# FFN up projection of a two-block model: weights or tokens as the standing operand

## The reference

```python
h = rms_norm(x, ln_ffn_pre[i])                 # (256, 2048)
g, u = jnp.split(h @ w_gate_up[i], 2, axis=-1) # w_gate_up: (2048, 2 * 5632)
f = (jax.nn.silu(g) * u) @ w_down[i]           # w_down: (5632, 2048)
x = x + rms_norm(f, ln_ffn_post[i])
```

## Time and profile before

| what | value |
|---|---|
| median of 3 runs | 2859.03 us (2858.27 to 2859.66) |
| the profiled execution's own time | 2858.7 us |
| its span in the profile | 2856.9 us |
| PE busy | 2817.7 us, 99% |
| PE weight loads (beside the matmuls) | 2400.2 us, 84% |
| DVE busy | 1732.5 us, 61% |
| ACT busy | 1284.7 us, 45% |
| GpSimd busy | 123.8 us, 4% |
| HBM read | 511.49 MB, 180 GB/s over the span |

### The profile page before, as it was taken

How to read it: one execution, slowest core, us unless ns; L and a number is a source line. 1 busy time by engine, 2 the same in 40 slices (tenths; PEclk the granted TensorE clock), 3 DMA queues, 4 the chain that set the end, 5 groups by cost and what they waited for, 6 DMA issues and landing times.

```text
span 2856.9 us, 40648 instructions
## 1 busy us (share of the span) xinstructions
PE 2817.7 (99%) x14485; PEld 2400.2 (84%) x14485; DVE 1732.5 (61%) x2253; ACT 1284.7 (45%) x1818; POOL 123.8 (4%) x129
## 2 busy tenths in 40 slices
PE   6999999999999999999999999999999999999999
PEld 3678888888888899988888999998888888888887
DVE  4468888888763366644456666675645555544465
ACT  3422224343352254434445677674544444444463
POOL 0000001001010000001112000000000000000000
PEclk9999999999999999999999999999999999999999
DMA  9765565445645245533335555555555555566655
GB/s 384 284 218 185 185 222 178 161 163 179 218 133 184 96 161 179 180 123 110 110 111 163 175 165 177 164 177 188 170 187 189 191 185 190 191 201 193 194 180 170
DMA packets 144780, 515.27 MB, mean 180 GB/s; under 512 B 16768, under 2 KB 16824, under 8 KB 142752
## 3 DMA queue, kind: packets, MB, share of 16 engines
q1 hardware_dynamic: 141408, 496.84, 52.2%
q0 software_dynamic: 3264, 16.94, 1.7%
HBM read 511.49 MB, written 2.22 MB: 180 GB/s over the span
## 4 chain that ended last, share of the span: by engine, by line
PE 95%; DVE 2%; ACT 1%; issue 1%; DMA 1%; POOL 0%; SPq 0%; DVEq 0%; ACTq 0%; POOLq 0%
PE main L1994 70%; PE main L1987 16%; PE aux L1941 2%; PE main L2300 2%; PE aux L2197 1%; PE aux L2188 1%; PE aux L2300 1%; PE aux L2316 1%; PE aux L2248 0%; DVE w_lo L1203 0%; DMA X<-in_xT 0%; PE main L2412 0%; DVE scores L1758 0%; DMA wide<-in_w_side 0%; PE aux L2200 0%
## 5 line engine op out<-in xcount | busy, mean ns | idle before, releaser
L1203 DVE TENSOR_TENSOR w_lo<-raw,w_hi 128x1024 fp32r<-128x1024 f32 (+1 forms) x768 | 924.4, 1206 | 768.2 <-ACT w_hi L677 759.2
L677 ACT ACTIVATE w_hi<-raw 128x1024 fp32r<-128x1024 f32 (+1 forms) x768 | 788.1, 1030 | 1180.3 <-PE main L1994 922.8
L1994 PE MATMUL main<-w_hi,act_hi 128*128 128x512 f32 (+1 forms) x1408 | 530.6, 377 | 2.9 <-DVE scores L1485 1.5
L1994 PE MATMUL main<-w_hi,act_lo 128*128 128x512 f32 (+1 forms) x1408 | 521.8, 371 | 0.0
L1994 PE MATMUL main<-w_lo,act_hi 128*128 128x512 f32 (+1 forms) x1408 | 521.5, 370 | 0.0
L1994 PE MATMUL main<-w_hi,h_all 128*128 128x512 f32 x1664 | 519.7, 391 | 0.9 <-ACT pp L1171 0.9
L1994 PEld LDWEIGHTS main<-w_hi,h_all 128*128 128x128 f32 x1664 | 312.4, 188 | 65.6 <-DVE h_all L1423 1.3
L1994 PE MATMUL main<-w_hi,quarters 128*128 128x384 f32 (+1 forms) x1280 | 357.6, 351 | 0.0
L1994 PE MATMUL main<-w_lo,h_all 128*128 128x512 f32 x832 | 323.8, 389 | 0.0
L1987 PE MATMUL main<-act_hi,w_hi 128*128 128x256 f32 (+1 forms) x928 | 308.3, 332 | 3.6 <-DVE act_lo L1326 2.3
L1987 PE MATMUL main<-act_lo,w_hi 128*128 128x256 f32 (+1 forms) x928 | 306.8, 331 | 0.0
(11 more groups left out here) (311 smaller groups left out, 2640.5 us busy)
## 6 DMA issues: line engine op xcount, KB each, us to landing
raw<-in_w_ffn_up SPq DMA_DIRECT2D x176, 512.0 KB, 3.5
raw<-in_w_in_ret SPq DMA_DIRECT2D x128, 512.0 KB, 4.2
gates<-in_w_side SPq DMA_DIRECT2D x124, 512.0 KB, 3.5
raw<-in_w_in_conv SPq DMA_DIRECT2D x116, 512.0 KB, 4.1
raw<-in_w_out SPq DMA_DIRECT2D x96, 512.0 KB, 3.7
raw<-in_w_ffn_down SPq DMA_DIRECT2D x88, 512.0 KB, 4.2
mod_raw<-in_w_mod SPq DMA_DIRECT2D x64, 512.0 KB, 8.5
raw<-in_w_sb SPq DMA_DIRECT2D x64, 384.0 KB, 3.2
```

The source lines that it names most:

```text
L677: A(w_hi[:, slot, 0:w], raw[:, slot, 0:w], ACT.Copy).then_inc(hi_split, 1)
L1203: V.tensor_tensor(out=w_lo[:, slot, 0:w], in0=raw[:, slot, 0:w], in1=w_hi[:, slot, 0:w].bitcast(F32), op=ALU.subtract).then_inc(lo_split, 1)
L1994: ins = mm(bank[:, c0:c1], x, w_part[:, slot, j * n + c0:j * n + c1], start=(k == 0 and j == 0 and i == 0), stop=(k == per - 1 and j == 1 ...
```

## The change

In `ffn_up` the weights stand. Each of 4 groups of 128 channels of a chunk has a PSUM bank. `w_hi` is loaded and the tokens' high and low parts (`h_pair`, 2 x 256 columns out of `h_all`) move past it in one matmul; `w_lo` is loaded and the high part alone (256 columns) moves past. The bank then holds high and low sums in two halves of 256 columns. A chunk uses all 4 `main` banks, the next one all 4 `aux` banks. The result lies by channel, as `ffn_down` needs it, and the transposes of the product are left out. DVE adds the two halves of each bank (`tensor_reduce`), multiplies gate and up by the token scale, which now differs along the columns; ACT takes Silu from SBUF; DVE multiplies gate and up; ACT and DVE split the product as before, from SBUF. The scales are spread over the columns once: DVE makes a diagonal of them in k = 6 of chunk 0, PE multiplies it with ones in k = 7, DVE copies the result to `room`. Two semaphores are renamed (`stats_done` and `act_pause` become `pause`), which the diff leaves out.

```diff
--- before.py
+++ after.py
@@ -67,7 +67,7 @@
 SIDE0_SLOTS = 4
 SUM_AT = 3
 
-LINKS = {..., 'dve_ffn_up': 0, ...}
+LINKS = {..., 'dve_ffn_up': 2, ...}
 
 COLS, _n = {}, 0
 for _name, _w in [("norm0", 16), ("norm1", 16), ("bmod0", 32), ("bside", 64), ("convw0", 24),
@@ -303,8 +303,9 @@
         late = ExitStack()
         frow = sb(late, "frow", [P, D])
         late.close()
-        fs = xs2[:, 0, :].rearrange("p (t n) -> p t n", t=2)
-        ff = xs2[:, 1, :].rearrange("p (t n) -> p t n", t=2)
+        halves = lambda ap: ap.rearrange("p (b n) -> p b n", b=2)
+        f_gate, f_up = xs2[:, 0, :], xs2[:, 1, :]
+        h_pair = h_all[:, 56:56 + 2 * KT * 256].rearrange("p (h k n) -> p h k n", h=2, n=256)
 
         main = [top.enter_context(nc.psum_tensor(f"main{i}", [P, 512], F32)) for i in range(4)]
         aux = [top.enter_context(nc.psum_tensor(f"aux{i}", [P, 512], F32)) for i in range(4)]
@@ -1000,16 +1001,11 @@
 
             def ffn_up(e, par, k):
                 if k == 0:
-                    act.wait_ge(eaten, chunk_end("ffn_up", e))
-                    act.wait_ge(s["norm_rstd"], 6)
-                    act.wait_ge(s["f_T"], e + 1)
-                    for t in range(2):
-                        ins = A(fs[:, t, :], main[2 * par + t][:, 0:256], ACT.Silu, scale=scale_h[:, t:t + 1])
-                    ins.then_inc(free_a, 1)
+                    act.wait_ge(s["f_done"], 2 * e + 2)
+                    A(f_gate, f_gate, ACT.Silu).then_inc(free_a, 1)
                 if k == 2:
-                    act.wait_ge(s["f_T"], e + 2)
-                    pause()
-                    A(f_hi[:, ds(e * 512, 512)], aux[0][:, :], ACT.Copy).then_inc(s["f_hi"], 1)
+                    act.wait_ge(s["f_done"], 2 * e + 3)
+                    A(f_hi[:, ds(e * 512, 512)], f_up, ACT.Copy).then_inc(s["f_hi"], 1)
 
             def gate(e, par, k):
                 if k == 0:
@@ -1671,16 +1667,35 @@
                     ins = V.scalar_tensor_tensor(out=x3[:, t, cs], in0=rr[:, t, cs], scalar=rstd[:, t:t + 1], in1=x3[:, t, cs], op0=ALU.mult, op1=ALU.add)
                 return ins
 
+            def ffn_row(k):
+
+                if k == 6:
+                    V.tensor_tensor(out=f_gate[:, 0:256].rearrange("p (t n) -> p t n", t=2), in0=mat("ident").unsqueeze(1).to_broadcast([P, 2, P]),
+                                    in1=scale_h[:, 0:2].unsqueeze(2).to_broadcast([P, 2, P]), op=ALU.mult).then_inc(s["f_done"], 1)
+                if k == 7:
+                    dve.wait_ge(s["rstd_row"], 1)
+                    V.tensor_copy(out=room[:], in_=aux[3][:, 0:256]).then_inc(s["f_lo"], 1)
+
             def ffn_up(e, par, k):
+                by_token = room[:].unsqueeze(1).to_broadcast([P, 2, 256])
                 if k == 0:
+                    dve.wait_ge(eaten, chunk_end("ffn_up", e))
+                    banks_of = main if par == 0 else aux
+                    for b in range(4):
+                        ins = V.tensor_reduce(out=xs2[:, b // 2, b % 2 * 256:b % 2 * 256 + 256], in_=banks_of[b][:, :].rearrange("p (h n) -> p n h", h=2),
+                                              axis=AX.X, op=ALU.add)
+                    ins.then_inc(free_d, 1)
+                    dve.wait_ge(free_d, done_d["ffn_up"] + e + 1)
+                    V.tensor_tensor(out=halves(f_gate), in0=halves(f_gate), in1=by_token, op=ALU.mult).then_inc(s["f_done"], 1)
+                    ch.link(V.tensor_tensor(out=halves(f_up), in0=halves(f_up), in1=by_token, op=ALU.mult))
+                if k == 1:
                     dve.wait_ge(free_a, done_a["ffn_up"] + e + 1)
-                    for t in range(2):
-                        ins = V.scalar_tensor_tensor(out=ff[:, t, :], in0=main[2 * par + t][:, 256:512], scalar=scale_h[:, t:t + 1], in1=fs[:, t, :], op0=ALU.mult, op1=ALU.mult)
-                    ins.then_inc(free_d, 1)
+                    V.tensor_tensor(out=f_up, in0=f_up, in1=f_gate, op=ALU.mult).then_inc(s["f_done"], 1)
+                    dve.wait_ge(s["f_done"], 2 * e + 3)
                 if k == 2:
                     dve.wait_ge(s["f_hi"], e + 1)
                     sl = ds(e * 512, 512)
-                    V.tensor_tensor(out=f_lo[:, sl], in0=aux[0][:, :], in1=f_hi[:, sl].bitcast(F32), op=ALU.subtract).then_inc(s["f_lo"], 1)
+                    V.tensor_tensor(out=f_lo[:, sl], in0=f_up, in1=f_hi[:, sl].bitcast(F32), op=ALU.subtract).then_inc(s["f_lo"], 1)
                     dve.wait_ge(s["f_lo"], e + 2)
 
             def gate(e, par, k):
@@ -1699,7 +1714,7 @@
                     dve.sem_inc(free_d, 1)
 
 
-            for n in ("side_T", "cv_done", "rt_y", "rt_sT", "a_y", "f_lo"):
+            for n in ("side_T", "cv_done", "rt_y", "rt_sT", "a_y"):
                 dve.sem_inc(s[n], 1)
             dve.sem_inc(free_d, 1)
             dve.sem_inc(s["side_used"], 3)
@@ -1914,7 +1929,12 @@
             dve.wait_ge(free_a, done_a["out2"] + 4)
             norm_sum(4, 2, rstd)
             dve.wait_ge(free_d, done_d["ffn_up"])
-            phase("ffn_up", lambda k: prepare(5, ln("ffnpre"), residual, k), ffn_up)
+
+            def ffn_start(k):
+                prepare(5, ln("ffnpre"), residual, k)
+                ffn_row(k)
+
+            phase("ffn_up", ffn_start, ffn_up)
 
             def down_step(e, par, k):
                 if e == 0 and k == 0:
@@ -1958,6 +1978,8 @@
                         pe.wait_ge(free_a, done_a[name] - (1 if by_last in by_act else 0))
                     else:
                         pe.wait_ge(free_a, (done_a[name] + c - back) if name in by_act else done_a[name])
+                if name == "ffn_up" and k == 0 and not isinstance(c, int):
+                    pe.wait_ge(s["f_lo"], 1)
                 pe.wait_ge(lo_split, BASE[name] + c * per + k + 1)
                 if name == "gate" and k == 0 and c < 2:
                     pe.wait_ge(s["pj_done"], 3 + c)
@@ -1978,6 +2000,20 @@
                             pe.wait_ge(s["half_a"] if t == 0 else free_a, a0 + before if t == 0 else done_a[name] + before)
                         else:
                             pe.wait_ge(s["half_d"] if t == 1 else free_d, d0 + before if t == 1 else done_d[name] + before)
+                    if name == "ffn_up":
+
+                        for j in range(2):
+                            kt, w0 = 2 * k + j, j * n + c0
+                            both = lambda: mm(bank[:, :].rearrange("p (h n) -> p h n", h=2), w_hi[:, slot, w0:w0 + P], h_pair[:, :, kt, 0:c1],
+                                              start=(first and j == 0), stop=(k == per - 1 and j == 1))
+                            high = lambda: mm(bank[:, 0:c1], w_lo[:, slot, w0:w0 + P], h_pair[:, 0, kt, 0:c1], start=False, stop=False)
+                            if j == 0:
+                                both()
+                                high()
+                            else:
+                                high()
+                                ins = both()
+                        continue
                     if isinstance(stat, int):
 
                         hi, lo, step = act_hi, act_lo, 512
@@ -2253,16 +2289,12 @@
                         ins = tr(aux[0][:, t * P:(t + 1) * P], on[:, t, :])
                     ins.then_inc(s["a_yT"], 1)
 
-            def ffn_up(e, par, k):
-                if k == 1:
-                    pe.wait_ge(free_d, done_d["ffn_up"] + e + 1)
-                    pe.wait_ge(s["f_lo"], e + 1)
-                    for j in range(2):
-                        for t in range(2):
-                            ins = tr(aux[0][:, (2 * j + t) * P:(2 * j + t + 1) * P], ff[:, t, j * P:(j + 1) * P])
-                    ins.then_inc(s["f_T"], 1)
-
-            pe.sem_inc(s["f_T"], 1)
+            def ffn_row(k):
+
+                if k == 7:
+                    pe.wait_ge(s["f_done"], 1)
+                    mm(aux[3][:, 0:256], mat("ones"), f_gate[:, 0:256], start=True, stop=True).then_inc(s["rstd_row"], 1)
+
             pe.sem_inc(s["side_sum"], 1)
 
             def first_sum():
@@ -2386,7 +2418,13 @@
             phase("sb", sb_start, sb_step, attn_parts)
             phase("dil", lambda k: head_steps(front, back, "sb", 7, 1, k), lambda e, par, k: head_steps(front, back, "dil", e, par, k), attn_parts)
             phase("out2", lambda k: last_head(front, back, nothing, k), lambda e, par, k: None, two(o_hi, o_lo), ready=lambda k: pe.wait_ge(s["p_lo_ready"], 16 + k + 1))
-            phase("ffn_up", norm_head(5, 2, None, "ffn_up", (12, 2)), ffn_up, two(g_hi, g_lo))
+            ffn_head = norm_head(5, 2, None, "ffn_up", (12, 2))
+
+            def ffn_start(k):
+                ffn_head(k)
+                ffn_row(k)
+
+            phase("ffn_up", ffn_start, lambda e, par, k: None, lambda par: [((main if par == 0 else aux)[b], b * P, 256, 0) for b in range(4)])
 
             def down_ready(k):
                 if k == 21:
@@ -2394,7 +2432,7 @@
                 elif k == 0:
                     pe.wait_ge(s["f_lo"], 22)
 
```

(12 more changed lines are left out.)

## The result

| | before | changed |
|---|---|---|
| median of 12 runs | 2858.6 us (2857.89 to 2859.93) | 2866.57 us (2864.69 to 2867.41) |
| the profiled execution's own time | 2858.7 us | 2864.69 us |
| its span | 2856.9 us | 2862.9 us |

The changed kernel is 8.0 us slower, ratio 1.0025 [1.0018, 1.0033]. The forecast was 2862.9 in a range of 2853 to 2875. The kernel before had medians between 2858.6 and 2859.6 in the four sets of runs. Its single executions differ by more: where the mean granted clock of one was 0.998 or 0.999 it mostly took 2858 to 2859 us, and at 0.996 about 2860, and the other kernels split alike, so a median shifts with how many executions fall on each side. I therefore read nothing from differences under 1 us between sets, and take the account of the time from the traces.

The account below looks back on a forecast made before the run. PE, 95% of the chain, was taken as the bound: -10.5 + 9.4 + 3.1 + 1.6 + 0.3 = +3.9 on the profiled 2858.7 us gives 2862.6, with 0.3 for the median 2862.9; range 2853 to 2875.

Parts of the forecast that it names:

- PE: the transposes go: FFN on PE: 22 groups of four transposes vanish, 0.479 us each, -10.5 us, all on the path.
- PE: the matmuls change shape: Up projection: 16 matmuls for 12 a piece, same columns, 226.7 and 120.0 ns each; +0.053 us a piece, +9.4 us.
- Rival 1: Up projection: long matmuls stay slow behind short ones, 232 to 235 ns; 2870 to 2875 us, slower; chance 0.28.
- rival 4: Up projection: short matmuls take only their columns, loads running over a long neighbour; 2844 us, faster; chance 0.06.
- rival 3: Up projection: the four more matmuls cost nothing beyond columns, a piece stays 2.720 us; 2853.5 us; chance 0.14.
- The moving operand in two runs: Up projection's matmuls: a moving operand in two runs of 256 columns, 4096 elements apart, costs nothing.
- DVE and ACT: Chunk's end: longer chain, reductions of 0.68 us, covered by three pieces split ahead with 1.6 us to spare; no cost.
- Rival 2: Chunk's end: slow DVE reductions, 1.37 us each, make PE wait at the fourth piece; +25 us, 2891 us; chance 0.08.
- The pause: Start of the down projection: PE waits longer for the last chunk's Silu, 1.51 us becoming some 4.6; +3.1 us.
- Half clock: Behind the pause before the down projection: clock falls once, eight matmuls lose 0.2 us each; +1.6 us, bounds 0 and twice that.
- The row of scales: Chunk 0, once: PE multiplies the token scales with ones in fp32, 256 columns; +0.3 us, PE not waiting.

Follow-up runs that it names:

- e4: Kernel before without the 22 groups of FFN transposes, the product split as it lies by token (values in wrong places): 2848.18 us, ratio 0.996.
- e7: Changed kernel with each piece's matmuls reordered to four long, eight short, four long, so runs of eight across pieces: 2867.31 us, one run.
- e8: Changed kernel with long and short matmuls in strict alternation, except one pair of each kind at a piece's edge: 2871.84 us, one run.
- e6: Changed kernel with the low weights also taking both token halves, so 16 matmuls of 512 columns a piece and none of 256: 3013.36 us, one run.
- e9: Changed kernel with DVE multiplying the gate by the token scale four more times, each waiting for the other: 2890.81 us, one run.
- e1: Changed kernel, but the down projection's first piece waits for the last chunk but one of ACT's Silu, not the last: 2859.45 us, ratio 0.9999.
- e10: Changed kernel itself, unedited, run again in a second set: 2865.76 us, ratio 1.0024.
- e3: Changed kernel with 36 idle 128-column fp32 matmuls filling the pause before the down projection: 2868.05 us, ratio 1.0028.
- e5: Changed kernel with 18 idle 128-column fp32 matmuls filling the pause before the down projection: 2862.86 us, ratio 1.0015.
- e2: Kernel before, with the down projection's first piece waiting for ACT's last chunk but one instead of the last: 2857.38 us, ratio 0.9994.

## Why the prediction came out as it did

**The total** was right within 4 us of 2866.6, and inside the range; what I gave as the likeliest, within 0.2%, was not met by the first set (8.0 us, where I had put the bound at 5.7) and just missed by the second (6.3). Against the profiled execution it was 2.1 us short (2862.6 forecast, 2864.7 measured), nearly all of it the matmuls' shape; the median lies 1.9 us above that execution, where I had put 0.3. The measured sign is a small loss, to which I gave 0.42.

**PE: the transposes go, -10.5.** Right: e4 measured -11.4 with 10.5 inside the interval.

**PE: the matmuls change shape, +9.4.** The mechanism, 16 loads and matmuls for 12 at an extra of 13.3 ns each, was right; the size was off, because I took 226.7 and 120.0 as additive. A piece took 2.786 us and not 2.773, which makes 176 x (2.786 - 2.720) = +11.6 instead of +9.4. It is the term that missed inside the stage. Rival 1's cause is real: the long ones never settle, at 233 ns. But its sum charged only the long ones; the short ones behind long ones come early (115 ns), which gives most of it back. Rival 1 held one side of the pair and rival 4 the other, in part: of the 13.3 ns that a short one costs beyond its columns, about 5 are gone behind a long one. Neither had the total: rival 1 as priced asked for 22.5 us a chunk, rival 4 for less than 21.6, rival 3 for 21.76, and 22.29 was measured. The gain was in the trace already: the first two of its twelve short ones take 114 and 119 ns. I read "no gain visible" from the sum over all twelve, where 7 ns vanish. e7 fits the forecast of its expectation; e8 does not fit its own, that single alternation costs what two and two costs; e6 shows that length and not the operand's layout is the cause. The rows show what a mixture costs, not why: in a run of eight the lateness is 27 ns over the first five long ones and the gain 7 over the first two short ones; two and two it is 13 and 10. What in PE makes the long one behind short ones late stays open.

Rival 3 does not hold: a piece would have stayed at 2.720 us, and the trace has 2.786; e6 shows 13.3 ns over the columns in the long form alone. By the formula in the Trainium skill, "TensorE: Matmul & The Clock Gate", section "Back-to-back issue gap", an estimate for a piece is 8 x (213.3 + 2.5) + 8 x (106.7 + 2.5) = 2.600 us. The trace does not agree, and I had used the formula beyond what the section gives it for: the gap of a single matmul. For streams of load and matmul the section states 131 ns at 512 columns, which no run here shows either.

**The moving operand in two runs, at no cost.** Right: e6 shows it.

**DVE and ACT.** Right. A reduction lasts 0.68 us as forecast, the fourth piece has 2.1 us to spare (1.6 forecast), and e9 shows both that the cover exists and where it ends. Rival 2's mechanism is the one that e9 sets off: its price was right, about a microsecond per chunk for each microsecond beyond the cover (e9), and only its condition, a slow reduction, does not hold.

**The pause, +3.1.** Right: 4.56 against 1.51. e1 shows its weight: with the pause away the time is that of the kernel before, since -10.5 + 11.6 and 0.4 for the row of scales make +1.5, and the 1.3 us of the old pause are saved as well.

**Half clock, +1.6.** Right in the profiled execution, too small for others: 2.3 in e10's. By the medians it is 1.5 to 4 us (e3, e5). I had seen one stretch of half clock in one trace and took its length as fixed. In the changed kernel it lasted 3.4 us in one execution and 6.8 in another, but 2 of the 6.8 lay in the pause and cost nothing; in e9, whose pause is longer, it was about 10, with half of it in the pause. In e6, e7 and e8, with the pause of 4.56 us, the matmuls behind it lost 1.6, 1.6 and 1.4 us. That the first profile showed just my 1.6 is luck: its mean granted clock, 0.997, occurs once in the 23 executions of the changed kernel, and e10's, 0.998, twelve times. The upper bound of twice the value, 3.2 us, covers every profile; what decides how long the half clock lasts stays open.

**The row of scales, +0.3.** The product appears as two matmuls where I had priced one at 0.26 us; they lie between 2037.90 and 2038.80 and cost 0.4 us. PE does not wait.

**The account of the profiled execution**: -10.5 + 11.6 + 3.05 + 1.6 + 0.4 = +6.15, and 0.1 less since the stage began earlier: 6.05, against 6.0 measured.

## What to carry to other kernels

When a change lengthens the chain from the last product of a stage to the first of the next, look first at what that first product really waits for: here the wait asked for one chunk more than the banks need, and narrowing it took away 6.7 us at no cost, more than the rest of the change moved. To judge what is left, give the kernel before the same repair: here the changed kernel is then still 1.5 to 2 us behind (e1 and e2). Price a PE pause of this length (4.6 us) as itself plus a stretch at half clock behind it, and keep a factor of two on that second term. Costs per matmul read from runs of one form are not additive when forms alternate; a piece of the exact mixture has to be measured, and the order within it counts for one per cent (22.29 against 22.56 us a chunk).

## What was not expected of the hardware

- Long (512) and short (256) matmuls, each with its own load, take 226.7 and 120.0 ns in runs of their own, 233 and 115 two and two, 235 and 117 one and one; in runs of eight the first five long ones are late by 27 ns together.
- A moving operand in two runs of 256 columns, 4096 elements apart, is as fast as one run: 226.7 ns.
- The half clock behind the same pause of 4.56 us began 1.0 us behind PE's first matmul in one execution and before it in another, and lasted 3.4 and 6.8 us, with 1.6 and 2.3 us lost.
- An fp32 product of 128 columns appears as two matmuls of 0.11 us each.
